# Interleaved reads of the moving weight chunks in a three-block float32 network on one core

## The reference

```python
for l in range(2):
    x = x + 0.5 * rms_norm(swiglu(rms_norm(x, g), w_gu, w_down), g2)     # 1024 -> 2 x 2816 -> 1024
    x = x + rms_norm(hybrid_mixer(rms_norm(x, g3), w_in, w_out, ...), g4)
    x = x + 0.5 * rms_norm(swiglu(...), g5)
# the second block, once
h = rms_norm_2(x, g)
y_ssm, y_conv, y_attn = ...            # from h @ w_in
x = x + (gates[0] * y_ssm + gates[1] * y_conv + gates[2] * y_attn) @ w_out
x = x + (silu(f_gate) * f_up) @ ffn_w_down
```

## Time and profile before

| What | Value |
|---|---|
| Median of 3 runs | 1448.06 us |
| Lowest and highest | 1447.97 and 1450.02 us |
| Span of the profiled execution | 1447.8 us |
| PE busy | 1425.5 us, 98% |
| DVE busy | 1153.4 us, 80% |
| ACT busy | 779.5 us, 54% |
| Read from HBM, over the span | 184 GB/s |

### The profile page before, as it was taken

The page is one execution under the profiler, slowest core; times in us unless marked ns, Lnnn a source line. Parts: engine busy times, 40 slices in busy tenths (PEclk is TensorE's granted clock), DMA queues, the critical chain, the costliest instruction groups (busy, mean ns, idle before and its releaser), DMA issues.

```text
span 1447.8 us, 24184 instructions
## 1 busy us (share of the span) xinstructions
PE 1425.5 (98%) x8485; PEld 1246.2 (86%) x8485; DVE 1153.4 (80%) x1832; ACT 779.5 (54%) x1242; POOL 143.1 (10%) x142
## 2 busy tenths in 40 slices
PE   8999999999999999999999999999999999999999
PEld 7888889888888888888988888888887899888887
DVE  5877777878777787777787988886999976587776
ACT  6444466664444644446667666566544465464442
POOL 0000005100000000001510000022133300000000
PEclk9999999999999999999999999999999999999999
DMA  8666655446665666665545666655634366566562
GB/s 323 217 190 188 194 158 178 156 154 210 197 191 189 213 216 189 193 193 156 180 152 181 206 228 220 218 169 181 219 117 138 110 179 187 174 190 191 187 200 75
DMA packets 73090, 268.05 MB, mean 185 GB/s; under 512 B 8240, under 2 KB 8240, under 8 KB 72752
## 3 DMA queue, kind: packets, MB, share of 16 engines
q1 hardware_dynamic: 69984, 253.79, 55.4%
q10 hardware_dynamic: 3024, 13.15, 2.5%
HBM read 262.71 MB, written 4.19 MB: 184 GB/s over the span
## 4 chain that ended last, share of the span: by engine, by line
PE 90%; DVE 6%; ACT 2%; issue 1%; POOL 1%; DMA 0%; DVEq 0%; ACTq 0%
PE work L777 25%; PE work L778 13%; PE acc L490 9%; PE acc L491 9%; PE acc L492 9%; PE work L490 8%; PE work L491 7%; PE work L492 7%; DVE wlo L476 2%; PE acc L1549 1%; ACT whi L469 1%; PE work L1521 1%; PE work L682 0%; PE acc L675 0%; PE work L1043 0%
## 5 line engine op out<-in xcount | busy, mean ns | idle before, releaser
L469 ACT ACTIVATE whi<-raw 128x1024 fp32r<-128x1024 f32 x480 | 496.9, 1049 | 417.6 <-PE work L778 233.4
L476 DVE TENSOR_TENSOR wlo<-raw,whi 128x1024 fp32r<-128x1024 f32 (+1 forms) x460 | 555.3, 1233 | 43.2 <-ACT whi L469 41.8
L777 PE MATMUL work<-xboth,whi 128*128 128x512 f32 x1600 | 552.3, 391 | 0.0
L778 PE MATMUL work<-xboth,wlo 128*128 128x256 f32 x1600 | 442.2, 276 | 0.0
L777 PEld LDWEIGHTS work<-xboth,whi 128*128 128x128 f32 x1600 | 300.4, 188 | 64.1
L778 PEld LDWEIGHTS work<-xboth,wlo 128*128 128x128 f32 x1600 | 300.4, 188 | 3.7
L490 PE MATMUL acc<-whi,hhi 128*128 128x512 f32 x440 | 173.2, 394 | 0.0
L491 PE MATMUL acc<-wlo,hhi 128*128 128x512 f32 x440 | 172.2, 391 | 0.0
L492 PE MATMUL acc<-whi,hlo 128*128 128x512 f32 x440 | 171.7, 390 | 0.0
L898 DVE TENSOR_REDUCE sg<-work 128x256 f32<-128x512 f32 x100 | 69.1, 691 | 78.6 <-PE work L778 78.5
L490 PE MATMUL work<-xboth,whi 128*128 128x256 f32 (+1 forms) x424 | 121.1, 286 | 0.0
(11 more groups left out here) (457 smaller groups left out, 2100.8 us busy)
## 6 DMA issues: line engine op xcount, KB each, us to landing
raw<-stream SPq DMA_DIRECT2D x480, 512.0 KB, 4.1
par<-pm ACTq DMA_DIRECT2D x2, 1644.5 KB, 7.6
spilled<-rotated ACTq DMA_DIRECT2D x6, 512.0 KB, 5.7
pfa<-pf_a ACTq DMA_DIRECT2D x3, 516.0 KB, 4.3
table<-spilled ACTq DMA_DIRECT2D x3, 512.0 KB, 3.2
par<-spilled ACTq DMA_DIRECT2D x3, 512.0 KB, 3.3
pfb<-pf_b ACTq DMA_DIRECT2D x2, 516.0 KB, 8.6
x<-x_in SPq DMA_DIRECT2D x2, 512.0 KB, 6.0
```

Of the source, the lines that this page charges most:

```text
L469: nc.scalar.activation(chunk(whi, place, c)[:, cols], chunk(raw, place, c)[:, cols], ACT.Copy).then_inc(hi_ready, 1)
L476: nc.vector.tensor_tensor(chunk(wlo, place, c)[:, cols], chunk(raw, place, c)[:, cols], chunk(whi, place, c)[:, cols].bitcast(F32), ALU.su ...
L777: nc.tensor.matmul(o[:, :], hi[:, k * P:(k + 1) * P], xboth[:, k, :], start=k == 0, stop=False)
L778: m = nc.tensor.matmul(o[:, 0:S], lo[:, k * P:(k + 1) * P], xhi[:, k, :], start=False, stop=k == KD - 1)
```

## The change

Every matrix whose chunks are a moving operand of 512 columns is permuted on the host: within each 512 columns first the 256 even ones, then the 256 odd ones (`weave`). On the chip the matmul reads such a run of 512 as `woven`: element 0 of the first half, element 0 of the second, element 1 of the first, and so on. The columns thus reach TensorE in their natural order, and the results stand in PSUM where they stood. In `head` the chunks are not permuted; there the moving operand takes one element of the gate chunk and one of the up chunk in turn, and so gate and up alternate in `W[t]`, and `pairs` is changed to read them. The 390-column run of the mixers, matmuls of 256 columns in the last mixer, and chunks that are the stationary operand are left as they are.

```diff
+        def woven(ap):
+
+            return ap.rearrange("p (a n) -> p n a", a=2)
+
...
-                    m = product(acc[:, t, halves_of(h)], *left(n, t), hi[:, halves_of(h)], lo[:, halves_of(h)], False, n == last)[-1]
+                    m = product(acc[:, t, halves_of(h)], *left(n, t), woven(hi[:, halves_of(h)]), woven(lo[:, halves_of(h)]), False, n == last)[-1]
...
         def pairs(o):
 
-            return o.rearrange("p (j s n) -> p j s n", j=2, s=2)
+            return o.rearrange("p (j n s) -> p j s n", j=2, s=2)
 
         def ffn_pe(pe, n, q, place, turns):
             def head(t):
                 hi, lo = [chunk(w, place, 0, 4).rearrange("p (c k n) -> p c k n", c=4, k=KD) for w in (whi, wlo)]
-                o = W[t][:, :].rearrange("p (c n) -> p c n", c=4)
+                o = W[t][:, :].rearrange("p (j m) -> p j m", j=2)
...
-                        recent += product(o[:, cs], xhi[:, k, t * P:(t + 1) * P], xlo[:, k, t * P:(t + 1) * P], hi[:, cs, k, :], lo[:, cs, k, :], k == 0, k == KD - 1)
+                        right = [w[:, cs, k, :].rearrange("p (j s) n -> p j n s", s=2) for w in (hi, lo)]
+                        recent += product(o[:, c // 2:(c + step) // 2], xhi[:, k, t * P:(t + 1) * P], xlo[:, k, t * P:(t + 1) * P], *right, k == 0, k == KD - 1)
...
                         m = product(acc[:, t, cols], hhi[:, j % 4, t * P:(t + 1) * P], hlo[:, j % 4, t * P:(t + 1) * P],
-                                    hi[:, cols], lo[:, cols], False, False)[-1]
+                                    woven(hi[:, cols]), woven(lo[:, cols]), False, False)[-1]
...
-                                      hi[:, k * n:(k + 1) * n], lo[:, k * n:(k + 1) * n], k == 0, k == KD - 1)
+                    right = [woven(w[:, k * n:(k + 1) * n]) if n == 2 * CW else w[:, k * n:(k + 1) * n] for w in (hi, lo)]
...
+def weave(w, n=512):
+
+    return w.reshape(w.shape[:-1] + (-1, n // 2, 2)).swapaxes(-1, -2).reshape(w.shape)
+
+
 def ffn_chunks(w_gu, w_down):
-    gate, up, down = channel_chunks(w_gu[:, :FF]), channel_chunks(w_gu[:, FF:]), w_down.reshape(FT, P, D)
+    gate, up, down = channel_chunks(w_gu[:, :FF]), channel_chunks(w_gu[:, FF:]), weave(w_down).reshape(FT, P, D)
```

More of the change, by code:

```diff
@@ L806, in first_down @@
                         m = product(acc[:, t, cols], hhi[:, 0, t * P:(t + 1) * P], hlo[:, 0, t * P:(t + 1) * P],
-                                    hi[:, cols], lo[:, cols], True, False)[-1]
+                                    woven(hi[:, cols]), woven(lo[:, cols]), True, False)[-1]
                 m.then_inc(consumed, 1)
@@ L994, in tokens @@
                             turn_scaled(pe, q, r, 1)
-                    recent += product(bank(name, slice(at, at + n)), xhi[:, k, t * P:(t + 1) * P], xlo[:, k, t * P:(t + 1) * P],
-                                      hi[:, k * n:(k + 1) * n], lo[:, k * n:(k + 1) * n], k == 0, k == KD - 1)
+                    right = [woven(w[:, k * n:(k + 1) * n]) if n == 2 * CW else w[:, k * n:(k + 1) * n] for w in (hi, lo)]
+                    recent += product(bank(name, slice(at, at + n)), xhi[:, k, t * P:(t + 1) * P], xlo[:, k, t * P:(t + 1) * P], *right, k == 0, k == KD - 1)
                     if padded and k == 0:
@@ L1108, in mix_pe @@
                         cols = slice(h * 512, (h + 1) * 512)
-                        m = product(acc[:, t, cols], *left(k, t), hi[:, cols], lo[:, cols], i == 0, False)[-1]
+                        m = product(acc[:, t, cols], *left(k, t), woven(hi[:, cols]), woven(lo[:, cols]), i == 0, False)[-1]
                 m.then_inc(consumed, 1)
@@ L1416, in tokens @@
                     recent += product(bank2(name, slice(at, at + n)), xhi[:, k, t * P:(t + 1) * P], xlo[:, k, t * P:(t + 1) * P],
-                                      hi[:, k * n:(k + 1) * n], lo[:, k * n:(k + 1) * n], k == 0, k == KD - 1)
+                                      woven(hi[:, k * n:(k + 1) * n]), woven(lo[:, k * n:(k + 1) * n]), k == 0, k == KD - 1)
                     if last:
@@ L1645, in mix2_pe @@
                         ms = product(acc[:, t, cols], mxhi[:, k, t * P:(t + 1) * P], mxlo[:, k, t * P:(t + 1) * P],
-                                     hi[:, cols], lo[:, cols], k == 0, False)
+                                     woven(hi[:, cols]), woven(lo[:, cols]), k == 0, False)
                         if k == 0 and t == 0 and h == 0:
@@ L2511, in mix_chunks @@
     gate, rec, z, xbc, dt, uv = np.split(w_in, cut, axis=1)
-    rows = w_out.reshape(KD, P, D)
+    rows = weave(w_out).reshape(KD, P, D)
     return (list(region(np.concatenate([z, dt], axis=1))) + [channel_chunks(xbc)[b] for b in XBC_ORDER] + list(channel_chunks(rec))
-            + list(channel_chunks(gate)) + [np.zeros((P, CH), w_in.dtype)] + list(region(uv)) + [rows[k] for k in OUT_ORDER])
+            + list(channel_chunks(gate)) + [np.zeros((P, CH), w_in.dtype)] + list(region(weave(uv))) + [rows[k] for k in OUT_ORDER])
 def per_partition(v):
@@ L2574, in mix2_chunks @@
     chunks.update(zip(D_B, b))
-    parts = list(region(q)) + twice + list(region(ng)) + [u[0], u[1], u[2]] + list(region(np.concatenate([ks, kw, vs, vw], axis=1))) + [u[3]]
+    parts = list(region(weave(q))) + twice + list(region(ng)) + [u[0], u[1], u[2]] + list(region(weave(np.concatenate([ks, kw, vs, vw], axis=1)))) + [u[3]]
     chunks.update(zip(W1_CHUNK, [c for i in range(2) for c in region(a["cmp_w1_2"][0, i])]))
@@ L2587, in mix2_chunks @@
     parts += [np.zeros((P, CH), w.dtype)]
[L2588 removed]
+    parts += list(weave(a["w_out_2"][0]).reshape(KD, P, D))
     assert len(parts) == MIX2_CHUNKS
```

## The result

| | Median | Lowest and highest | Runs |
|---|---|---|---|
| Before | 1448.01 us | 1447.91 and 1450.02 | 4 |
| Changed | 1424.36 us | 1421.27 and 1424.97 | 4 |

The medians differ by 23.7 us, 1.6%; the ratio over all the runs is 0.983, with a 95% interval from 0.9819 to 0.9842. The forecast was 1418 us in a range from 1410 to 1465.

A forecast was written before the change was run, and what follows sets the result against it. TensorE was taken as the bound, busy 98% of the span, with float32r matmuls slowed by their moving operand's fetch. 32.0 us of PE time, less 5% waited away, gave 1448 - 30 = 1418 us; range 1410 to 1465 without rival (a).

The forecast's parts named there:

- Count and target of the read: 1992 matmuls of 512 columns and 96 of 256 on weights change; each 512 falls from 230 or 236 to 216 ns.
- Sum: All woven matmuls: 18.5 + 10.1 + 2.4 + 1.0 = 32.0 us of PE time, 30 us after 5% off for mixer waits.
- the 504 matmuls on `xboth`: Woven matmuls with `xboth`, each falling from 236 to 216 ns: 10.1 us of the saving.
- The base: Whole kernel: profiled span 1447.8 us against a median of 1448.06, the 0.3 us difference taken as within the runs' spread.
- a change in 777 and 778: Sign of being wrong: these untouched FFN matmuls leave 340 ns a pair, so the woven operand's read isn't what counts.
- The heads' readers: Lines 846 and 886 now read every second element: no cost taken, at most 9 us for the range.
- The reason that I gave: Moving-operand fetch from SBUF loses one step per 64 bytes; with two streams in turn each 64 bytes last twice as long.
- the sixteenth: Contiguous float32r matmuls: a pair of 777 and 778 takes 340 ns, 17/16 of the 320 ns for its 768 columns.
- Rival (a): All 1992 woven matmuls pay one access an element, 420 ns instead of 230 to 236: 375 us more, 1823 us; chance 0.20.
- (b): Woven matmuls lose only the part above 17/16 and fall to 227 ns: 9.4 us saved, 1439 us; chance 0.20.
- (c): No effect on woven matmuls, the port's rate being fixed in bytes: within 3 us of 1448; chance 0.12.
- (d): Woven reads meet weight loads more often, every woven matmul takes 240 ns: 17 us more, 1465 us; chance 0.08.

The follow-up runs named there:

- `after_again`: The changed kernel run once more with nothing altered; measured 1424.63 us, its profiled run 1421.48 us.
- `e1_near`: The changed kernel with the two streams of the FFN down projections 2, 4, 8 or 16 elements apart, by block; measured 1427.28 us.
- `e9_repeats`: The changed kernel with FFN down projections reading only some weights, each several times over, in four orders without alternation; measured 1421.67 us.

## Why the prediction was right

- **Count and target of the read.** The step "I take 216" came true to the nanosecond, on `acc` and on `work`, for all operand pairs. It was taken from line 1053, where eight records of plain float32 start 216 ns apart; that such a record stands for 512 columns was an assumption. That bound was the useful part: it tells what a perfect fetch would give, without knowing why the fetch is late. That the woven read would reach it was partly luck. The evidence was VectorE's read of PSUM, and the forecast got 0.40; of the orders tried later, four streams in turn (512 bytes apart) and A A B B A A B B (1024) also take places far apart in turn, and they are slower than contiguous.
- **Sum.** 32.0 us of PE time were forecast, less about 2 us waited away in the mixers. Between the profiled executions without a 350 ns FFN (before, and `after_again`) PE's busy time fell by 30.3 us (1425.5 to 1395.2) and its idle time grew by 2.3 (22.3 to 24.6), so the span fell by 28.0 (1447.8 to 1419.8). The FFNs gave 3.7 us each as worked out, 18.5. The term that was too large is the one of the 504 matmuls on `xboth`, 10.1 us: it takes 236 ns for all three lines of `product`, and the third line had less to lose. Its mean duration fell by 12 ns (392 to 380), while those of the first two fell by 17 and 18, which makes some 1.3 us over its 168 matmuls.
- **The base.** This step was wrong by some 1.5 us. I took the span of 1447.8 as belonging to the median run, 0.3 us below it. In each run where both are known the time is 1.7 to 1.8 us over the span (1424.97 and 1423.3; 1421.48 and 1419.8; 1399.09 and 1397.4). So the profile of before came from an execution of about 1449.5 us, 1.5 over the median. In which of its parts the 1.5 us lie isn't known, and sets of runs differ by nearly as much: the kernel before has medians of 1448.01, 1448.30 and 1449.04 us in three of them.
- **Not foreseen.** In most runs of the changed kernel one FFN has the 350 ns pairs, 3 us. 1418 + 2 (sum) + 1.5 (base) + 3 (350 ns pairs) = 1424.5, and 1424.36 was measured. In the three runs that seem to be without them, 1421.27 to 1421.86 us, the forecast is off by 3 to 4. The prediction has a change in 777 and 778 among its signs of being wrong. The sign came, in one FFN, but it did not mean what was said there: the woven matmuls were at 216 ns all the same.
- **The heads' readers.** Nothing, as taken; the bound of 9 us was not needed. The Trainium skill ("SBUF — State Buffer", the note on cachelines) gives PSUM lines of 8 bytes and says that patterns that aren't contiguous slow down matmuls; the prediction stretched this to the readers. It does not bind ScalarE or VectorE here: 473 and 421 ns with a stride of two, 475 and 421 without. ScalarE's idle time before `whi` fell, as forecast, from 417.6 us to 401.3.
- **The reason that I gave.** Half right. That the interval hangs on how long a piece serves, and that two streams give each piece twice the time, is what `e1_near` and `e9_repeats` show. That the piece has 64 bytes, drawn from the sixteenth, is wrong: it has 16, and by the pair model the sixteenth is 1.77 ns against the 1.67 of two pairs.
- **Rival (a), one access an element.** It fell, but not far off: its 420 ns are what a single stream with a step of 8 to 32 bytes pays (430 to 459). The rule of the Trainium skill behind it, "SBUF — State Buffer", the note on cachelines, has the line of 16 bytes right, as `e1_near` shows. At least two hits in a row are neither needed nor enough: with alternating lines there is never a hit in a row and the interval is 216 ns, and one stream over every second element hits each line twice in a row and takes 455. Here two pairs of reads between changes are a little too few (227 to 236 ns) and four are enough (216).
- **Rivals (b), (c), (d).** The intervals went to 216 ns, below the 227 of (b), the 230 to 236 of (c) and the 240 of (d), so both the sixteenth and the part that depended on operands went.

## What to carry to other kernels

Where TensorE is the bound and the moving operand is float32r, compare the interval between matmul starts at full clock with columns / 2.4 GHz; if it is a sixteenth or more above, try reading the operand as two contiguous streams in turn, at least 16 bytes apart, and put the order right on the host or in the engine that reads the result. Don't give such an operand a step of 8, 16 or 32 bytes in a single stream (430 to 460 ns instead of 216), and do not take four streams for two. When a change touches one kind of matmul, look for the same loss in the others: here the ones left alone were worth another 25 us. Other data types were not tried.

## What was not expected of the hardware

- The interval of a matmul with a float32r moving operand hangs on how often the 16-byte piece changes: 216 ns for 512 columns when a piece serves for eight reads, alone or in turn with another one read by read, 227 to 236 for four in a row, 430 to 459 with a change at every read or every second one. The pair model (reads in pairs of 0.83 ns, at least 1.77 ns from one change to the next, both members of a pair may bring a new piece at once) fits eight of the orders in the table (one of them, 430, to 5%), and gave the four of `e9_repeats` beforehand. It is not shown as the mechanism: it does not give the 330 ns of A A B B A A B B nor the 268 and 282 of four in turn (453 by the model; perhaps something of earlier pieces is kept), nor the 251 of alternating groups of four (227 by the model). These are open.
- The same contiguous matmuls can run at 350 instead of 340 ns a pair, a whole FFN long in one execution and not in the next, or block by block, as the read order of the matmuls just before has it. Two profiles of one program are needed before a difference of 3 us in 1424 is put down to a change.
- Each operand pair had its own excess before (230, 236 ns), and none with woven reads. The part that weight loads have in this was not tried.
